# A three-block layer stack on one core: norms, bias table, index scores and the picks of two masks behind single slabs of block 1's projection, low parts in quarters

## The reference, cut to what matters

```python
xn = _rms_norm(h, mix_norm[l])
proj = xn @ w_in[l]
attn_cols, rwkv_cols, gate_cols = _split(proj, (ATTN_IN, RWKV_IN, GATE_IN))
q, k, v, q_idx, k_idx, w_idx = _split(attn_cols, ATTN_SPLITS)
q = _rms_norm(q.reshape(B, S, ATTN_HEADS, ATTN_HEAD_DIM), attn_q_norm[l])
k = _rms_norm(k.reshape(B, S, ATTN_HEADS, ATTN_HEAD_DIM), attn_k_norm[l])
...
head_scores = jax.nn.relu(jnp.einsum('bqhd,bsd->bqhs', qib, k_idx32) * IDX_DIM ** -0.5)
scores = jnp.einsum('bqhs,bqh->bqs', head_scores, wib) * IDX_HEADS ** -0.5
scores = jnp.where(causal[None], scores, -jnp.inf)
_, sel = lax.top_k(scores, topk)
...
bias = rel_bias32[_t5_bucket(q_pos[None, :, None] - sel)]
logits = logits + jnp.transpose(bias, (0, 3, 1, 2))
probs = jax.nn.softmax(logits, axis=-1).astype(v.dtype)
return jnp.einsum('bhqk,bqkhd->bqhd', probs, v_sel)
```

## Time and profile before

| | |
|---|---|
| median of three runs | 3141.22 us (3140.93 to 3146.04) |
| the profiled execution | 3141.03 us, span of its trace 3139.2 us |
| mean granted clock of TensorE | 0.967 of full speed |
| busy: TensorE | 2950.8 us (94% of the span) |
| busy: VectorE | 1418.2 us (45%) |
| busy: ScalarE | 1151.5 us (37%) |
| busy: GpSimd | 1195.4 us (38%), of it 442 low parts 1096.1 us |
| HBM | 90 GB/s over the span |

### The profile page before, as it was taken

The page is one execution under the profiler, slowest core; times in us unless marked ns, Lnnn a source line. Parts: engine busy times, 40 slices in busy tenths (PEclk is TensorE's granted clock), DMA queues, the critical chain, the costliest instruction groups (busy, mean ns, idle before and its releaser), DMA issues.

```text
span 3139.2 us, 39978 instructions
## 1 busy us (share of the span) xinstructions
PE 2950.8 (94%) x15600; PEld 2314.3 (74%) x15600; DVE 1418.2 (45%) x2023; ACT 1151.5 (37%) x1678; POOL 1195.4 (38%) x557
## 2 busy tenths in 40 slices
PE   7989988999999999899999999999999887999998
PEld 6855647868888886767888888767777576888886
DVE  4007756465221373523265443333287543674442
ACT  4243352354222335334342223444443524442222
POOL 4422521134444452433544444423323222544442
PEclk9998989999999999999999999999999899999999
DMA  4322210043233332224422222312212103522222
GB/s 136 99 74 65 71 34 2 2 155 94 95 100 94 108 129 77 95 91 154 155 95 100 94 94 94 114 61 78 81 51 84 54 29 107 192 94 96 99 94 81
DMA packets 80667, 284.07 MB, mean 90 GB/s; under 512 B 8968, under 2 KB 9096, under 8 KB 79744
## 3 DMA queue, kind: packets, MB, share of 16 engines
q1 hardware_dynamic: 66240, 236.36, 22.9%
q10 hardware_dynamic: 13296, 41.97, 3.5%
q0 software_dynamic: 976, 3.56, 0.4%
HBM read 260.86 MB, written 20.99 MB: 90 GB/s over the span
## 4 chain that ended last, share of the span: by engine, by line
PE 39%; issue 36%; POOL 16%; DVE 5%; ACT 3%; DMA 1%; POOLq 0%; ACTq 0%; SPq 0%; DVEq 0%
POOL slab_r L2929 15%; PE bank L360 10%; PE bank L362 10%; PE bank L361 10%; PE bank L609 2%; DVE work L2368 1%; PE bank L586 1%; DVE small L2366 1%; PE bank L663 1%; DVE work L2355 1%; PE bank L493 1%; PE bank L503 0%; PE bank L950 0%; PE bank L676 0%; PE bank L692 0%
## 5 line engine op out<-in xcount | busy, mean ns | idle before, releaser
L2929 POOL TENSOR_TENSOR slab_r<-slab,slab_high 128x1024 fp32r<-128x1024 f32 x442 | 1096.1, 2482 | 1610.2 <-ACT slab_high L1200 1603.1
L360 PE MATMUL bank<-xh,slab_high 128*128 128x512 f32 x2256 | 904.1, 401 | 31.8 <-POOL slab_r L2929 26.9
L362 PE MATMUL bank<-xh,slab_r 128*128 128x512 f32 x2256 | 884.8, 392 | 0.0
L361 PE MATMUL bank<-x_raw_r,slab_high 128*128 128x512 f32 x2064 | 810.6, 393 | 0.0
L1200 ACT CAST slab_high<-slab 128x1024 fp32r<-128x1024 f32 x442 | 461.9, 1046 | 445.2 <-DMA slab<-in_w_down 215.6
L361 PE MATMUL bank<-work_r,slab_high 128*128 128x512 f32 x1376 | 543.6, 395 | 0.0
L360 PEld LDWEIGHTS bank<-xh,slab_high 128*128 128x128 f32 x2256 | 428.2, 190 | 143.4 <-POOL slab_r L2929 25.9
L362 PEld LDWEIGHTS bank<-xh,slab_r 128*128 128x128 f32 x2256 | 427.5, 190 | 92.5
L360 PE MATMUL bank<-work_r,slab_high 128*128 128x512 f32 x1184 | 470.3, 397 | 22.6 <-DMA cst<-in_cst 15.5
L362 PE MATMUL bank<-work_r,slab_r 128*128 128x512 f32 x1184 | 473.7, 400 | 0.0
L361 PEld LDWEIGHTS bank<-x_raw_r,slab_high 128*128 128x128 f32 x2064 | 391.9, 190 | 80.4 <-issue 1.9
(11 more groups left out here) (464 smaller groups left out, 2841.5 us busy)
## 6 DMA issues: line engine op xcount, KB each, us to landing
slab<-in_w_down SPq DMA_DIRECT2D x88, 512.0 KB, 3.2
slab<-in_w_up SPq DMA_DIRECT2D x64, 512.0 KB, 3.2
slab<-in_w_gates SPq DMA_DIRECT2D x56, 512.0 KB, 3.3
slab<-in_w_merge SPq DMA_DIRECT2D x48, 512.0 KB, 4.0
slab<-in_w_gu SPq DMA_DIRECT2D x44, 512.0 KB, 3.5
slab<-in_w_in_a SPq DMA_DIRECT2D x32, 512.0 KB, 3.5
gates<-staging ACTq DMA_DIRECT2D x56, 256.0 KB, 3.6
slab<-in_w_out SPq DMA_DIRECT2D x24, 512.0 KB, 3.3
```

The costliest lines, as they stand in the source:

```text
L360: first = pe.matmul(bank[b][:, :], wh, mh, start=start, stop=False)
L361: pe.matmul(bank[b][:, :], wh, ml, start=False, stop=False)
L362: end = pe.matmul(bank[b][:, :], wl, mh, start=False, stop=stop)
L2929: pool.tensor_tensor(slab_low[:, slot, :], slab[:, slot, :], plain(slab_high[:, slot, :]), ALU.subtract).then_inc(S("slab_split"), 1)
```

## The change

Four things change.

1. Only slabs 4 to 7 of the projection stay in the loop (`A_ALONE = 8`). Slabs 8 to 31 are written out one by one on TensorE and ScalarE, and behind each stands a piece of the small work: the table's matmuls behind slab 8, two norm sums behind each of 9 to 12, two flips behind each of 13 to 16, 8 turns of values behind 15 and 16, the turn of the index weights behind 18, two index scores behind each of 18 to 29. The first `logits` stands ahead of slab 31. ScalarE has its pieces in the same places.
2. The tiles are computed in another order (`A_TILES`): 30 and 31 come before 16 to 29.
3. VectorE does 4 rounds of picks behind every second index score from mask 2 on: those of mask 1 while the scores of mask 2 are added up, those of mask 2 during mask 3's. Only mask 3's 16 rounds are left in attention, one a step.
4. GpSimd makes each low part in four instructions of 256 columns instead of one of 1024; only the last raises `slab_split`. This holds for all 442 slabs.

```diff
-        TOPK_STEPS = 6
...
+        A_TILES = list(range(16)) + [30, 31] + list(range(16, 30))
+        A_ALONE, A_SUMS, A_FLIPS, A_VALUES, A_SCORES = 8, range(9, 13), range(13, 17), (15, 16), range(18, 30)
+        PICKS, PICKS_ALONE = TOPK // 8, 4
...
+        scored = []
...
             entry("in_a")
-            dense("in_a", 32 - RING, DC, xnk, ["act"], xn_split)
...
+            dense("in_a", A_ALONE - RING, DC, xnk, ["act"], xn_split)
...
+            def slab_alone(b):
+
+                slot = slabs[0] % RING
+                slabs[0] += 1
+                pe.wait_ge(S("slab_split"), slabs[0])
+                pe.wait_ge(*last[b])
+                for k in range(DC):
+                    at = slice(k * P, (k + 1) * P)
+                    one, ins = product(b, (slab_high[:, slot, at], slab_low[:, slot, at]), xnk(k), k == 0, k == DC - 1)
+                    if k == 0:
+                        one.then_inc(begun, 1)
+                ins.then_inc(psum_for["act"], hand(b, "act"))
...
+            def index_score(i, h):
+
+                r = slice(HD * (h % 2), HD * (h % 2) + HD)
+                pe.wait_ge(*last[4 + h % 2])
+                pe.matmul(bank[4 + h % 2][:, 0:(i + 1) * P], W(12 + h // 2)[r, i * P:(i + 1) * P],
+                          W(30)[r, 0:(i + 1) * P], start=True, stop=True)\
+                    .then_inc(psum_for["act"], hand(4 + h % 2, "act"))
+                scored.append(handed["act"])
```

The order on TensorE:

```diff
+            for p in range(A_ALONE, 32):
+                if p == 31:
+                    mark("attention")
+                    logits(0)
+                slab_alone(p % RING)
+                if p == A_ALONE:
+                    bias_table()
+                if p in A_SUMS:
+                    c = 2 * A_SUMS.index(p)
+                    for e in range(2):
+                        sum_tiles([W(48 + c + e)], 4 + e, "act", pair, S("qk_square"))
+                if p in A_FLIPS:
+                    if p == A_FLIPS[0]:
+                        pe.wait_ge(S("table_back"), n.next(S("table_back"), 16))
+                    c = 2 * A_FLIPS.index(p)
+                    flips((c, c + 1))
+                    if p == A_FLIPS[-1]:
+                        mark("flipped")
+                if p in A_VALUES:
+                    if p == A_VALUES[0]:
+                        pe.wait_ge(S("qk_normed"), n.next(S("qk_normed"), 8))
+                    for e in range(2):
+                        t = 2 * A_VALUES.index(p) + e
+                        turn([(W(8 + c)[:, t * P:(t + 1) * P], c * P) for c in range(4)], 4 + e, "act")
+                if p in A_SCORES:
+                    if p == A_SCORES[0]:
+                        pe.wait_ge(*last[A_TILES.index(31) % RING])
+                        turn([(W(31)[:, t * P:(t + 1) * P], t * P) for t in range(NT)], 4, "dve")
+                    g = 2 * A_SCORES.index(p)
+                    for e in range(2):
+                        index_score(1 + (g + e) // 8, (g + e) % 8)
...
-            logits(0)
```

ScalarE, from the same place on:

```diff
+            copy_tiles("in_a", A_ALONE - RING, W3(RING, A_ALONE - RING))
...
+            def bias_table():
+
+                for o, b, w in ((W(57), 6, T), (W(58), 7, P)):
+                    act.wait_ge(psum_for["act"], n.next(psum_for["act"]))
+                    act.copy(o[0:8, 0:w], bank[b][0:8, 0:w]).then_inc(evac, n.up(evac))
+                act.wait_ge(evac, n.own(evac))
+                act.dma_start(a["scratch"], work[0:8, 57 * T:57 * T + NREL]).then_inc(S("table_out"), 16)
...
+            def index_relu(g):
+
+                i, h = 1 + g // 8, g % 8
                 act.wait_ge(psum_for["act"], n.next(psum_for["act"]))
...
+                if g >= 2:
+                    act.wait_ge(S("relu_used"), n.next(S("relu_used")))
+                act.activation(W(55 + h % 2)[:, 0:(i + 1) * P], bank[4 + h % 2][:, 0:(i + 1) * P], ACT.Relu)\
+                    .then_inc(evac, n.up(evac))
...
+            for p in range(A_ALONE, 32):
+                high_next()
+                act.wait_ge(psum_for["act"], n.next(psum_for["act"]))
+                act.copy(W(A_TILES[p]), bank[p % RING][:, :]).then_inc(evac, n.up(evac))
+                if p == A_ALONE:
+                    bias_table()
+                if p == A_ALONE + 1:
+                    act.wait_ge(S("table_out"), 16)
+                    act.dma_start(W3(40, 8), bass.AP(tensor=a["scratch"].tensor, offset=0,
+                                                     ap=[[1, P], [NREL, 8], [1, T]])).then_inc(S("table_back"), 16)
+                if p < A_ALONE + 4:
+                    for c in (2 * (p - A_ALONE), 2 * (p - A_ALONE) + 1):
+                        act.activation(W(48 + c), W(c), ACT.Square).then_inc(S("qk_square"), n.up(S("qk_square")))
+                if p in A_SUMS:
+                    c = 2 * A_SUMS.index(p)
+                    for e in range(2):
+                        bias, scale = (eps[6.4e-05], 1.0) if c < 4 else (eps[1e-06], 1.0 / HD)
+                        act.wait_ge(psum_for["act"], n.next(psum_for["act"]))
+                        act.activation(W(48 + c + e), bank[4 + e][:, :], ACT.Ln, bias=bias, scale=scale)\
+                            .then_inc(evac, n.up(evac))
+                if p == A_SUMS[-1] + 1:
                     act.wait_ge(evac, n.own(evac))
...
+                        act.activation(W(48 + c), W(48 + c), ACT.Exp, scale=-0.5)\
+                            .then_inc(S("qk_rstd"), n.up(S("qk_rstd")))
+                if p in A_FLIPS:
+                    for e in range(2):
+                        act.wait_ge(psum_for["act"], n.next(psum_for["act"]))
+                        act.copy(W(40 + 2 * A_FLIPS.index(p) + e), bank[6 + e][:, :]).then_inc(evac, n.up(evac))
+                if p in A_VALUES:
+                    if p == A_VALUES[0]:
+                        act.wait_ge(S("qk_normed"), n.next(S("qk_normed"), 8))
+                    for e in range(2):
+                        act.wait_ge(psum_for["act"], n.next(psum_for["act"]))
+                        act.copy(W(48 + 2 * A_VALUES.index(p) + e), bank[4 + e][:, :]).then_inc(evac, n.up(evac))
+                if p in A_SCORES:
+                    for e in range(2):
+                        index_relu(2 * A_SCORES.index(p) + e)
```

VectorE:

```diff
+                dve.wait_ge(evac_by["act"], scored[8 * (i - 1) + h])
+                if h == 0:
+                    dve.tensor_scalar(sc, W(55)[:, 0:w], SM(210 + 8 * i), None, ALU.mult)\
+                        .then_inc(S("relu_used"), n.up(S("relu_used")))
+                else:
+                    dve.scalar_tensor_tensor(sc, W(55 + h % 2)[:, 0:w], SM(210 + 8 * i + h), sc, ALU.mult, ALU.add)\
+                        .then_inc(S("relu_used"), n.up(S("relu_used")))
+                dve.wait_ge(S("relu_used"), n.own(S("relu_used")))
+                if h == 7:
+                    dve.tensor_tensor(sc[:, i * P:w], sc[:, i * P:w], C("caus"), ALU.add).then_inc(chain, n.up(chain))
+                    dve.wait_ge(chain, n.own(chain))
+
...
+            def top_k(i, rounds):
+
+                w = (i + 1) * P
+                sc = work[:, mask_at[i]:mask_at[i] + w]
+                for _ in range(rounds):
...
+                    dve.max(SM(250, 8), sc).then_inc(chain, n.up(chain))
+                    dve.wait_ge(chain, n.own(chain))
+                    dve.match_replace(sc, SM(250, 8), sc, PICKED).then_inc(chain, n.up(chain))
+                    dve.wait_ge(chain, n.own(chain))
+                picked[i] += rounds
+                if picked[i] == PICKS:
+                    dve.tensor_scalar(sc, sc, PICKED / 3 * 2, NEG, ALU.is_gt, ALU.mult)\
+                        .then_inc(S("mask_ready"), n.up(S("mask_ready")))
+                    dve.wait_ge(S("mask_ready"), n.own(S("mask_ready")))
+
+            for g in range(0, 8 * (NT - 1), 2):
+                i, h = 1 + g // 8, g % 8
+                add_score(i, h)
+                add_score(i, h + 1)
+                if i > 1:
+                    top_k(i - 1, PICKS_ALONE)
...
-                top_k(g)
+                if picked[NT - 1] < PICKS:
+                    top_k(NT - 1, 1)
```

GpSimd, and the order of the slabs in memory:

```diff
                         pool.wait_ge(S("slab_high"), i * RING + (s0 + j + 1))
-                        pool.tensor_tensor(slab_low[:, slot, :], slab[:, slot, :], plain(slab_high[:, slot, :]),
-                                           ALU.subtract).then_inc(S("slab_split"), 1)
+                        for q in range(4):
+                            at = slice(q * SLAB * P // 4, (q + 1) * SLAB * P // 4)
+                            low = pool.tensor_tensor(slab_low[:, slot, at], slab[:, slot, at],
+                                                     plain(slab_high[:, slot, at]), ALU.subtract)
+                            if q == 3:
+                                low.then_inc(S("slab_split"), 1)
```

```diff
-    A["w_in_a"] = _slabs(tiles, 1)
+    A["w_in_a"] = _slabs(tiles[:16] + tiles[30:] + tiles[16:30], 1)
```

116 lines of the change are left out of this document (16 added, 100 removed).

## The result

| | before | after |
|---|---|---|
| median, us | 3142.34 (3140.93 to 3146.04, 4 runs) | 3088.47 (3080.77 to 3092.51, 4 runs) |
| profiled execution, us | 3141.03 | 3085.53 |
| span, us | 3139.2 | 3083.7 |

The ratio is 0.9824, with a 95% interval of 0.9801 to 0.9847. The change was forecast at 34 us and brought 54 between the medians. The changed kernel was timed in two more sets, with medians of 3085.01 (5 runs) and 3091.33 (5 runs), so one median of it is good to about 3 us to either side.

The account below looks back on a forecast made before the run. TensorE was taken as the bound over most of the span, but waiting on ScalarE before attention and mostly on VectorE in attention. 3141.0 - 28.5 - 10.1 + 5 = 3107.4 us; 8-in-10 range 3096 to 3125.

Parts of the forecast that it names:

- A: Projection of block 1 up to attention's first turn of probabilities: small work behind single slabs gains 28.5 us.
- B: Attention: without the picks of masks 1 and 2, steps run at TensorE's own pace; gain 10.1 us.
- C: Low parts in quarters, all 442 slabs: net cost 5 us, bounds -5 and +12.
- rival 2: Behind the single slabs ScalarE or VectorE does not keep up, four slabs late by 2.5 us each: 3117, chance 0.12.
- three passes, not four: Index scores before attention: a pair of heads partly overlaps and costs three passes, 11.6 us for all 24.
- six at 0.5 and three at 1.5: TensorE's waits for low parts: six lengthen by 0.5 us and three by 1.5 through quarters, part of C's cost.
- Rival 1: Quarters alternate with VectorE's two-input instructions, low part 5.1 us; at ten of twelve waits C is 27: 3129, chance 0.12.
- Rival 3: C is a gain, since freed VectorE chains bind before 1300 and between 2260 and 2360 us: 3098, chance 0.09.
- Rivals 4 and 5: 4: GpSimd bounds full stretches, 3150, chance 0.02. 5: small work waits, TensorE stands behind slab 13, 3138, chance 0.02.
- First turn at 234.5: Sign for A: attention's first turn of probabilities comes at about 234.5 us instead of 263.
- 31 intervals in 146 to 149: Sign for B: attention's 31 intervals between steps take 146 to 149 us.
- The kernels' difference at 430 and at the end within 12 us of each other: Sign for C: it is wrong if the kernels' time gap at 430 us differs from that at the end by over 12.

Follow-up runs that it names:

- e8_scores_in_a_row: Changed kernel with picks of masks 1 and 2 back in attention and the 24 index scores in one row behind slab 30; row took 24.6 us, one run.

## Why the prediction was wrong

The sum missed the profiled execution by 21.9 us (3107.4 against 3085.53). A has 4.4 of them. B has 6.2, of which 5.5 are a miscount. C has 11.3, of which 3.6 lie behind attention and are within the spread: it was booked as a loss, and in the runs the quarters gained. So two steps of the prediction failed, the count in B and the sign of C. With the count alone put right the forecast would have been 3101.9, and the measured time would still lie below the range of 3096 to 3125.

**A, 28.5 forecast, 32.9 measured.** The mechanism was right in every part. TensorE was full from 60 to 230 us at the full clock but for one wait of 0.3 us, and waited for no low part there, so rival 2 did not occur. The terms of the sum were a little too high one by one. A pair of index scores holds TensorE for 0.63, 0.85 and 1.06 us (207.23 to 208.28), 10.2 for all instead of 11.6: two heads overlap more at the full clock than "three passes, not four". The return behind them costs 0.24, 2.9 in all instead of 3.6. The table's two matmuls take 1.17 with 0.14 behind, not 1.7; in the 1.7 read from the earlier trace rows was the 0.36 for which TensorE waited on ScalarE. Written-out slabs run at 0.2274 a matmul (e8_scores_in_a_row) where the loop's were at 0.2268, which costs 0.3 instead of 0.9. The norm sums come as forecast: 1.32 for a pair (98.28 to 99.60) and some 0.44 in the slab behind it, against 2 x 0.86. Together these make 3.1. Of the rest, 1.1 come ahead of slab 8, which begins at 64.39 instead of 65.52; three traces of the changed kernel have it at 63.86 to 64.76, and quarters alone at 64.69.

**B, 10.1 forecast, 16.3 measured by itself.** This step failed by counting. The prediction says "31 intervals between steps in 157.2 us" and sets 145.6, the sum over 31 steps at TensorE's pace, against it. But 420.16 in the earlier trace rows is the turn of the 31st step, not of the 32nd, which stands at 424.62. From 262.99 to 420.16 there are 30 intervals. With the same paces, 7 x 3.88 + 8 x 4.41 + 8 x 4.93 + 7 x 5.46 is 140.1 and the gain 17.1, less the 1.5 left for a late scaling 15.6. The wrong count put a whole step, 5.46 us, on the wrong side. The run with whole low parts has B without the quarters: 140.9 us for the 30 intervals, a gain of 16.3. So B with the right count would have been within 0.7. The change's own 138.2, which makes 19.0 in the table, needs the quarters; then no step waits, and the paces are 3.84, 4.38, 4.92 and 5.45, lower at each change of block.

The step whose clock had fallen (8.30 us) was not seen: its price lies within the 157.2, so it did not enter the sum wrongly, but the prediction took all of it for VectorE's work. Before the clock fell at 375 us, TensorE had waited for VectorE's scaling 1.58 us at 366.69 and 1.94 at 373.88. With quarters alone five waits are left of 13 and the step takes 5.13. That the waits lowered the clock is what this suggests; it isn't shown beyond that, and a wait of 2.30 at 290.02 was followed by no fall.

**C, +5 forecast, a gain measured.** This step failed by its sign. Quarters alone brought 7.4 us between medians, clear of the noise and below the bound of -5 that the prediction gave C. In the changed kernel they brought 5.5 between the medians of one chip, with sets of runs that overlap; against the changed kernel's other two medians it is 2.0 and a loss of 0.9. The gain is in attention: 9.9 us for quarters alone, 2.7 of the 19.0 beside the moved picks. The prediction saw that a scaling took 1.96 instead of 0.29 beside a low part, and booked no gain for it in attention: B's sum has every step at TensorE's pace already. That B reaches this pace only with quarters shows in the run with whole parts. The term "six at 0.5 and three at 1.5" can't be told from nothing: behind attention the kernels with quarters took 2721.4 against 2718.5, and 2714.9, 2718.1 and 2720.4 against 2715.4, so 2.9 more and on average 2.4 more, at the size of the spread. A low part became 3.17 us long on average, counted from its first quarter's start to its last one's end, where it had been 2.48; 0.6 had been estimated and 0.7 came. TensorE's waits for low parts grew from 29.3 to 32.0 us.

**The rivals.** Rival 1, the bad bargain, had the right mechanism in it and the wrong price. Where VectorE works beside, a quarter can take 1.18 us instead of 0.74, so turns do alternate. But only 52 of the 442 low parts take 3.9 us or more; 7 of them stand before one of the 17 waits, and all waits together grew by 2.7 us, not by 22. The Trainium skill (SBUF — State Buffer, Who interferes with whom) says the one that has the ports keeps them for its whole instruction. The trace agrees: the scaling at 259.72 with whole parts began 0.23 us behind a low part and ended 0.15 behind its end, after 2.32 us, and with quarters it takes 0.66. The prediction had put 3129 to that rule; the rule says who waits, and the profile has to say whether anyone waits for that one. The Trainium skill (Perfetto Trace Analysis, Per-engine timelines) calls GpSimd's spans unreliable and asks for start-to-start spacing. Here the two nearly agree: where VectorE is idle beside, most quarters have a span of 0.74 us and the next one starts 0.70 behind. Rival 3 had the right side and came nearest, 3098. It put the surplus where VectorE's chains bind ahead of 1300: some 4 us net did come there, between 1234 and 1314 us, and in the run with quarters alone too, but they were given back behind 2080, and most of the surplus was in attention. Rivals 4 and 5 did not occur.

**The range.** It was worked out from the unknown prices, with C between -5 and +12. A range of B's own counting was not in it, and this alone was over 5 us, and neither were A's 4.4 and the quarters' gain in attention.

**What the profile was to show.** First turn at 234.5: it came at 230.06. 31 intervals in 146 to 149: 31 took 142.6 (230.06 to 372.64), and the 30 of the table 138.2. Low parts of 0.7 to 0.75: most, with a mean of 0.82. No scaling above 1.3: one of 1.50, the others up to 1.28. All of those above 1.1 stand beside GpSimd's bias and not beside a quarter, where the longest is 0.89. The kernels' difference at 430 and at the end within 12 us of each other: 52.0 and 55.5. This last sign was met although C had the wrong sign, because it looks only behind attention and the quarters' gain lies inside.

## What to carry to other kernels

Before a stretch is divided into steps, find the first and the last step's rows and count the rows between them; a step too many is a whole step's error in the gain. An engine's short matmuls that wait for another engine are worth moving between full work not only for their waits but for the clock, which fell to 0.50 in such a row here, behind idle stretches in one kernel and behind 12 full slabs in another. And where a consumer needs a producer's result piece by piece, cutting the producer's instruction is only half of it: a semaphore step for every piece was worth 13 to 20 us here, the cutting itself 7 in the kernel before and at most 5.5 in the changed one. When one engine is seen to hold up another, book the gain of ending that as well as its price.

## What the runs showed that was not expected

- Two fp32 matmuls of 512 columns on different halves of the rows, one for each head, hold TensorE for 1.06 us together, where one over all rows takes 0.66 (two in 1.32).
- The clock can fall to 0.50 inside a stretch in which TensorE is shown busy for 3 to 5 of every 5 us: in attention of the kernel before, at 375 us, after waits of 1.58 and 1.94 us in the 10 us before.
- The slab behind a pair of fp32 norm sums takes 5.89 us, the one behind index scores 5.68, and a slab behind another 5.46. The price of going back to slab matmuls depends on what stood before.
- A kernel whose instructions are the same differs from itself by up to 6 us between the spans of two traces, at a few places of 1.5 to 7 us in either direction; at one of them the granted clock stood at 0.50 for 17 us in one trace and for 31 in the others.
- Halves do for attention what quarters do (134.97 against 135.00 us), though a scaling beside a half takes 1.2 us and beside a quarter 0.66: a wait has to fit into the step, it need not be as short as it can be.
